# Sixty-four spare bytes in the on-chip memory map of a two-block decoder kernel

## The reference

```python
q = (t @ w_q).reshape(n_tok, 8, 2, 128)
s_top, i_top = lax.top_k(sc, 16)           # sc = q against 128 keys, twice
best, pos = lax.top_k(cand, 16)            # of the 16 x 16 sums
g = jax.nn.softmax(best, axis=-1)
act = gelu(einsum("td,thkd->thk", t, u_tab[idx]))
out = einsum("thk,thkd->td", g * act, v_tab[idx])
```

## The kernel before

| tensors, in order | start of the first, bytes | modulo 128 |
|---|---|---|
| xT, h_hi, h_lo, prm | 1152 | 0 |
| cst, ring, ring_hi, ring_lo | 26816 | 64 |
| arena (the working area of 128 KB) | 65728 | 64 |
| wf, w_hi, w_lo | 196800 | 64 |
| xs_lo | 214464 | 64 |

## Time and profile before

### The profile page before, as it was taken

How to read it: one execution, slowest core, us unless ns; L and a number is a source line. 1 busy time by engine, 2 the same in 40 slices (tenths; PEclk the granted TensorE clock), 3 DMA queues, 4 the chain that set the end, 5 groups by cost and what they waited for, 6 DMA issues and landing times.

```text
span 2035.6 us, 37757 instructions
## 1 busy us (share of the span) xinstructions
PE 1988.1 (98%) x14131; PEld 1843.6 (91%) x14131; DVE 1508.9 (74%) x2593; ACT 1013.5 (50%) x1358; POOL 0.2 (0%) x4
## 2 busy tenths in 40 slices
PE   7999999999999999999999999999999999999998
PEld 6988999999999888888799999999999998888886
DVE  5767768887886666666679666688878866666666
ACT  3641454455555444444546554444555554444444
POOL 0000000000000000000000000000000000000000
PEclk9999999999999999999999999999999999999999
DMA  7655767776556777778655655777766667787786
GB/s 272 197 202 188 279 198 241 232 233 207 183 181 212 241 241 241 242 239 242 204 165 156 188 158 158 232 234 232 233 206 186 187 219 237 241 241 240 241 243 190
DMA packets 135164, 440.82 MB, mean 217 GB/s; under 512 B 14992, under 2 KB 15248, under 8 KB 131472
## 3 DMA queue, kind: packets, MB, share of 16 engines
q1 hardware_dynamic: 117200, 406.84, 64.5%
q10 hardware_dynamic: 17856, 32.51, 4.4%
HBM read 403.64 MB, written 35.65 MB: 216 GB/s over the span
## 4 chain that ended last, share of the span: by engine, by line
PE 90%; DVE 5%; DMA 3%; ACT 1%; issue 1%; SPq 0%; DVEq 0%; ACTq 0%
PE ps L561 27%; PE ps L563 27%; PE ps L562 27%; PE ps L855 3%; DVE ring_lo L374 2%; PE ps L598 1%; DMA arena<-in_w_ada 1%; DMA ring<-in_down 1%; PE ps L704 1%; PE ps L831 1%; ACT ring_hi L368 1%; PE ps L554 0%; DVE arena L1855 0%; PE ps L784 0%; PE ps L955 0%
## 5 line engine op out<-in xcount | busy, mean ns | idle before, releaser
L374 DVE TENSOR_TENSOR ring_lo<-ring,ring_hi 128x1024 fp32r<-128x1024 f32 x632 | 772.9, 1224 | 311.1 <-ACT ring_hi L368 308.4
L368 ACT ACTIVATE ring_hi<-ring 128x1024 fp32r<-128x1024 f32 x632 | 667.7, 1057 | 634.4 <-PE ps L563 509.0
L561 PE MATMUL ps<-h_hi,ring_lo 128*128 128x256 f32 x2816 | 803.8, 285 | 20.0 <-DVE ring_lo L374 9.5
L562 PE MATMUL ps<-h_lo,ring_hi 128*128 128x256 f32 x2816 | 791.5, 281 | 0.0
L563 PE MATMUL ps<-h_hi,ring_hi 128*128 128x256 f32 x2816 | 791.4, 281 | 0.0
L561 PEld LDWEIGHTS ps<-h_hi,ring_lo 128*128 128x128 f32 x2816 | 534.4, 190 | 25.1 <-issue 20.6
L563 PEld LDWEIGHTS ps<-h_hi,ring_hi 128*128 128x128 f32 x2816 | 536.5, 191 | 0.0
L562 PEld LDWEIGHTS ps<-h_lo,ring_hi 128*128 128x128 f32 x2816 | 534.3, 190 | 0.4 <-issue 0.2
L561 PE MATMUL ps<-ring_hi,w_lo 128*128 128x512 f32 x1024 | 398.4, 389 | 0.0
L562 PE MATMUL ps<-ring_lo,w_hi 128*128 128x512 f32 x1024 | 398.3, 389 | 0.0
L563 PE MATMUL ps<-ring_hi,w_hi 128*128 128x512 f32 x1024 | 398.3, 389 | 0.0
(11 more groups left out here) (284 smaller groups left out, 1289.2 us busy)
## 6 DMA issues: line engine op xcount, KB each, us to landing
ring<-in_down SPq DMA_DIRECT2D x256, 512.0 KB, 4.3
ring<-in_up SPq DMA_DIRECT2D x256, 512.0 KB, 4.1
ring<-in_w_in SPq DMA_DIRECT2D x80, 512.0 KB, 3.7
kept_z<-wf ACTq DMA_DIRECT2D x124, 256.0 KB, 3.2
xT<-kept_z SPq DMA_DIRECT2D x124, 256.0 KB, 4.3
arena<-in_w_ada SPq DMA_DIRECT2D x24, 1024.0 KB, 9.7
ring<-in_wq SPq DMA_DIRECT2D x32, 512.0 KB, 4.1
ring<-in_w_out_ssd SPq DMA_DIRECT2D x8, 512.0 KB, 3.8
```

What stands on the lines that cost most here:

```text
L368: nc.scalar.activation(ring_hi[:, part_slot(m), :], ring[:, slot(m), :], ACT.Copy).then_inc(S("high"), 1)
L374: ns.tensor_tensor(ring_lo[:, part_slot(n), :], ring[:, slot(n), :], ring_hi[:, part_slot(n), :].bitcast(fp32), ALU.subtract)\
L561: mm(psum, s_lo, m_hi, start=start, stop=False)
L562: mm(psum, s_hi, m_lo, start=False, stop=False)
```

## The change

One unused tensor of 64 bytes in each partition is declared between the rings and the arena.

```diff
@@ -97,6 +97,7 @@
         ring = sb("ring", [P, RING, BLK])
         ring_hi = sb("ring_hi", [P, RING, BLK], fp32r)
         ring_lo = sb("ring_lo", [P, RING, BLK], fp32r)
+        sb("between", [P, 16])
         arena = sb("arena", [P, 32768])
         wf = sb("wf", [P, 2, 512])
         w_hi = sb("w_hi", [P, 2, 512], fp32r)
```

## The result

The changed kernel is slower. Its median is 2045.25 us (2037.79 to 2050.31, 4 runs) against 2018.7 us (2016.76 to 2027.71, 4 runs) for the kernel before; the ratio is 1.0112, with a 95% interval of 1.0075 to 1.0149. The forecast was 1995 us, and the range ended at 2021.

What follows compares the result with a forecast made beforehand. TensorE was taken to bound the kernel, an up pass lasting its matmuls' number times pitch. Gains of 20.5 us (up) and 2.6 us (xs), 23.1 us off 2018.2, gave 1995 us; range 1988 to 2021 us.

Steps and rivals of the forecast that it cites:

- Step (1): Whole kernel: an address offset of 64 bytes adds no instruction, wait or transfer; 0 us.
- Step (2): Up passes, 512-column matmuls: pitch falls from 226.67 to 220.0 ns at distance 64, gaining 20.5 us.
- "0 gained": Up passes: the lower bound set on the up stream's gain; the upper was 41 us.
- The slower one: Up passes: distance 64 is bad with operands' sides changed, 233.3 ns, 20.5 us more, 2036 us; chance 0.08.
- The unmoved pitch: Up passes: 226.67 ns is already the floor, one cycle in sixteen; only xs gains, 2016 us; chance 0.35.
- The inference behind step (2): SBUF: a matmul's read and a weight load's collide if both want the same half of a 128-byte stretch.
- Step (3): Second mixer's scaled blocks, 576 xs matmuls of 256 columns: shorter pitch than 120.0 ns, 2.6 us gained.
- Steps (4) to (6): Plain fp32 matmuls reading arena: 0 us; DVE and ACT: hidden behind TensorE; up-pass block parts: 2.9 us slack, 0.16 taken.
- The two rhythms of the h stream: Mixer and down pass, 256 columns 64 apart: two steady pitches, 113.33 and 117.78 ns, picked by how the stream started.
- my own sign: In the profile after, the h stream must read as before, 113.33 and 117.78 ns, else the reading of two rhythms was wrong.

Runs made afterwards that it cites:

- e3: The kernel before with 64 spare bytes behind the arena, so only the coefficients and what follows them move; 2037.85 us against 2027.38, one run each.
- e5: The kernel before with 64 spare bytes ahead of everything the rings and coefficients follow, so both move; 2045.52 us in one run against 2027.38.

## Why the prediction was wrong

**What bounds the kernel: right.** The up pass lasts as long as its matmuls' pitch says, before and after, and nobody keeps TensorE waiting.

**Step (1), nothing is issued: right.** The instruction counts are equal.

**Step (2), the up stream: this step failed.** It said that the up stream at distance 64 gets what the h stream has, 16 cycles over its columns, and priced that at 20.5 us less. It has 48 cycles, 233.33 ns instead of 220.0, and costs 20.5 us more (3072 x 6.67). Two thoughts in the step have to be kept apart. That 32 cycles at distance 0 are a cost per matmul and not one cycle in sixteen was right (173.3 ns at 384 columns). That the gain from 64 bytes carries over from 256 to 512 columns was wrong, and no row of before spoke for it. At distance 0 I had two numbers of columns, at 64 only one, and I took the cost at 64 to be independent of the columns because the cost at 0 was. I also held "0 gained" for the lower bound in that step, and put the loss off into a rival.

The trace of before had a row that I didn't use. The plain fp32 matmuls of L784 move 2 columns each, with one load of 128 columns, and still start 112 ns apart. The columns can't be what sets that pitch, and the load may well be. The h stream's 113.33 ns lie 1.3 above it. Its 16 cycles over the columns may be the load and not a cost of the distance, and then they couldn't be carried over to 512 columns. That isn't shown: those loads are of plain fp32, and no run varied the load beside 256 columns.

**The rivals.** The slower one had the outcome and the very size of the pitch: 233.3 ns, 20.5 us. That the size fitted is luck, since its reason fell. Its 2036 us lie 9 us below the median of 2045.25: up and xs together explain 19.4 us, the medians differ by 26.6 and the ratio's interval is 15 to 30 us, and the h stream's rhythm alone can move an execution by more than the rest. The rival had a chance of 0.08, and its reason, that the operands change sides, was wrong: with 256 columns and the same sides 64 is the better distance (115.6 against 120.0 ns). The unmoved pitch and its floor of one cycle in sixteen fell at 384 columns. The range left out the one rival with a loss although no row excluded it.

**The inference behind step (2).** I wrote that two reads may want the same half of a 128-byte stretch. 128 is refuted: with 128 spare bytes the loss stays (1.0116, interval 1.0094 to 1.0138), with 256 it is gone (0.9983). The rest of the picture, two reads that meet, is not shown. The half loads speak for a part of the stationary side in it, but a picture that gives more with half a load than with a whole one I don't have.

**Step (3), the xs stream: right in sign.** The rhythm is the slow one, 117.5 ns between the two rows and 118.02 in the mean; about 1 us less, where I took 2.6. The same distance gave 116.78 in e3, with both rhythms in it.

**Steps (4) to (6): right.** The plain fp32 matmuls of L831, which the change moves from 0 to 64 apart, keep their pitch of 113.0 ns. L609 tells nothing of the change, since `cact` and the arena both move. `w_lo` still takes 693 ns, and ACT still waits for TensorE. No effect of the arena shows: e3 has the whole up loss without moving it, and e5 moves it and keeps the up pitch.

**The two rhythms of the h stream: half right.** They are two steady states, and an uninterrupted stretch keeps the one it has. I did not see that the pick changes between executions, so I took the 19 us between the profiled execution and the median for a constant. By my own sign, that the h stream must read as before, this reading failed. Most of the 19 us is the first halves of the two down passes at 117.78, about 7 us each; the second halves have 117.7 in every profile. Nor is the pick all chance: from the second group of L855 on it is always the slow rhythm, and behind the six matmuls of L875 it was the fast one even in the first profile (46 matmuls at 113.4 ns).

The rule of the Trainium skill, page "SBUF — State Buffer", section "Who interferes with whom", that TensorE's two read ports are independent and it waits on no one, does not give these times: by it addresses should not matter, and here 64 bytes of distance move the pitch by up to 6.7 ns with 256 columns, downwards, and by 6.7 ns with 512, upwards. Whether it is at those ports that the time is lost, no run here shows.

**Open.** The mechanism behind the distance, and why the cost at a distance grows with the columns; why half a load costs more at distance 0; what picks the rhythm of the h stream where nothing stands before it but its own kind (its mean pitch of 114.8 to 117.0 ns at an unchanged distance is some 18 us between executions); whether the loads into the rings take part; and the clean odd multiples of 16 bytes.

## What to carry to other kernels

In a stream that is bound by fp32r matmuls, compare the addresses of the two operands modulo 256, and measure the pitch for the number of columns that you use: a distance that is good for 256 columns was the worse one for 512. Two streams of one trace that differ in the distance alone settle the shape that they have, and for another shape they give a place to look, but no sign. When two profiles differ by less than such a change of rhythm can make, compare the streams' pitches and not the spans.

## What was unexpected of the hardware

- The place of an unused tensor changes the time by 1.1%, through the distance of two operands modulo 256: 226.7 ns at 0, 256 and 512, and 232.9 to 234.3 on average at 32, 64, 96, 128 and 192, for fp32r matmuls of 512 columns with loads of 128.
- With 256 columns 64 is better than 0: 120.0 ns at 0, and 113.3 or 117.8 at 64.
- The same program runs a stretch of 1726 matmuls of 256 columns, about 200 us, at 113.3 or at 117.8 ns from end to end, and not the same one in each execution (spans of 2035.6 and 2017.8 us). Between repeated groups of eight fp16 matmuls the pitch is 117.6 to 117.8 in every profile.
- Loads of 64 columns instead of 128 beside 512-column matmuls make the pitch longer, 230.0 against 226.7 ns.
